# Modulation as columns, later modulation loads first, every second low part's sum on GpSimd: the start of a retention / attention / expert layer

## Chip, cores and metric

One core of one Trainium2 chip. The metric is the device time of one execution in microseconds; for the kernel before the change the median of three runs is given. TensorE is the matrix engine, VectorE, ScalarE and GpSimd (POOL in the profile) are the others, and SyncE (SP) issues most of the loads.

## What is computed

One layer over 512 latent tokens and 256 context tokens of width 1024: adaptive norm, one projection into retention and differential attention, gated merge, then a top-4-of-32 mixture of experts. The change touches only its first lines:

```python
mod_l = (jax.nn.silu(c) @ w_mod + b_mod)[:, None, :]        # c: (1, 1024), w_mod: (1024, 6144)
mod_c = (jax.nn.silu(c_ctx) @ w_mod + b_mod)[None, None, :]
sh_a, sc_a, g_a, sh_f, sc_f, g_f = jnp.split(mod_l, 6, axis=-1)
csh_a, csc_a, ... = jnp.split(mod_c, 6, axis=-1)
hl = _rmsnorm(x, norm1_g) * (1.0 + sc_a) + sh_a             # 512 rows
hc = _rmsnorm(ctx, norm1_g) * (1.0 + csc_a) + csh_a         # 256 rows
... = _project(hl, w_in); ... = _project(hc, w_in)          # everything else hangs on these
```

## The kernel before, in words

All values are float32. Large products are made from split operands: ScalarE rounds a tile to a high part (`whi` of weights, `hhi` of activations), VectorE subtracts it from the tile to get the low part (`wlo`, `hlo`), and TensorE adds high by high, high by low and low by high. `hhi` and `hlo` hold the normed, modulated activations, transposed: eight chunks k of 128 channels, 768 token columns each.

The engines run their own programs, which are written out by hand and tied by semaphores. There is no planner: the order in each engine's program is the order of the work. The start-up goes like this.

- **SyncE** loads the conditioning vectors and the identity, then four pieces of `w_mod` (`load_mod`, L563; a piece is 512 rows by 512 columns, 1 MB; two pieces make 512 columns of shift or scale), then six tiles of x and the context (`load_x`, L568). Then come the first query weights (`load_qk(0, 0)`, issued at L550), pieces 4 to 7 (each waits until the product four earlier has freed its buffer), the first key weights, and a piece for the later modulation vectors (L580).
- **TensorE** (`mod_product`, through the helper `mm` at L2089) makes each piece's product with the two conditioning columns `ct` as the stationary operand and 512 columns of `w_mod` moving: four matmuls into a 2x512 row pair, in full float32, so that the trace shows two records for each. After products 0 to 3 it transposes four tiles of x (`turn_x_tile`, L2193: eight 128x128 transposes a tile). Then it turns the first half of the modulation (`turn_mod`, L2201: eight transposes of 2x128), makes product 4, transposes the last two tiles, makes products 5 to 7, and turns the second half. After that it starts the first query projection (`head_qk(0, 0)`). This asks for the first low weights (`lo_made`) and, chunk by chunk, for `h_lo`: six matmuls a chunk.
- **VectorE** scales the tiles of x (`x_norm`, L1372), adds the bias to the product rows (`mod_row`, L1368) and copies the turned columns into `mcols` (`mod_columns`, L1419 and L1420). For each chunk k it makes scale times x plus shift in full precision (L1431, two instructions: 512 latent and 256 context columns) and subtracts the high part (L1435). Between the two halves of four chunks it makes the low part of the first weights (`lo`, L1345).
- **ScalarE** makes the sums of squares (L939), copies the transposed x out (L945), makes `hhi` (L965, L967) and the high weights (L929).
- **GpSimd** loads the bias and the norm's weights at the start, makes the reciprocal roots (L772, L774), then issues the loads of constants (`more_inputs`, L752 to L761: 0.9 MB and many small ones), and clears an accumulator once all eight `h_lo` are made (L783).

Products alternate between the first four channel chunks (products 0 to 3) and the last four (4 to 7); each half needs a shift pair and a scale pair.

Of the kernel before, what the change touches and what calls it, by code (L numbers as in the profile page):

```python
# [27 lines left out]
ALU = mybir.AluOpType  # L28
# [3 lines left out]
P = 128  # L32
D = 1024
KC = D // P
L = 512
# [202 lines left out]
def build(nc, a, scratch):  # L238
    mod_d, h2_d, list_d, acc_d, accr_d = scratch
    ctx = ExitStack()  # L240
    with ctx:
# [57 lines left out]
        mod_turned = sem("mod_turned")  # L299
# [17 lines left out]
        mod_rows = sem("mod_rows")  # L317
# [219 lines left out]
        def _(sp):  # L537
# [54 lines left out]
            load_qk(0, 0)  # L592
            for j in range(MOD_SLOTS, MOD_N):
                load_mod(j)
            load_qk(0, 1)
# [136 lines left out]
        def _(pool):  # L732
# [44 lines left out]
            for k in range(3):  # L777
                pool.wait_ge(x_sq, 2 * k + 2)
                rstd(ss[:, 2 * k:2 * k + 2], 2, D, st, out=rs[:, 2 * k:2 * k + 2], m0=2 * k).then_inc(x_rstd, 1)
            more_inputs()  # L780
            pool.wait_ge(mod_vec, 2)
# [554 lines left out]
        def _(dve):  # L1336
# [26 lines left out]
            bm = F(A_BMOD, MOD_A, COL)  # L1363

            def mod_row(n):
                c = MOD_COLS[n]
                dve.wait_ge(mod_used, 2 * n + 2)
                V.tensor_tensor(bm[0:2, c, :], ps[0:2, c, :], bm[0:2, c, :], ALU.add).then_inc(mod_rows, 1)  # L1368

# [45 lines left out]
            def mod_columns(n):  # L1415
                ks = slice(KH * n, KH * n + KH)
                dve.wait_ge(mod_turned, n + 1)
                turned = ps[:, 3 * n, 0:4 * KH].rearrange("p (s k a) -> p s a k", s=2, a=2)
                V.tensor_copy(mcols[:, 0:4:2, ks], turned[:, 0])  # L1419
                V.scalar_tensor_tensor(out=mcols[:, 1:4:2, ks], in0=turned[:, 1], scalar=1.0,  # L1420
                                       in1=mcols[:, 4, ks].unsqueeze(1).broadcast_to((P, 2, KH)),
                                       op0=ALU.add, op1=ALU.mult).then_inc(mod_vec, 1)
# [3 lines left out]
            def h_low(k):  # L1426
                xt = F(A_XT, KC, T)[:, k, :]
                if k >= 2:
                    dve.wait_ge(h_lo, k - 1)
                for s, (n0, n1) in enumerate(((0, L), (L, T))):  # L1430
                    st.did(V.tensor_scalar(tm[:, k % 2, n0:n1], xt[:, n0:n1],  # L1431
                                           mcols[:, 2 * s + 1, k:k + 1], mcols[:, 2 * s, k:k + 1], ALU.mult, ALU.add))
                dve.wait_ge(h_hi, k + 1)
                st.wait()
                V.tensor_tensor(hlo[:, k, :], tm[:, k % 2, :], hhi[:, k, :].bitcast(F32), ALU.subtract).then_inc(h_lo, 1)  # L1435
# [4 lines left out]
            mod_row(0)  # L1440
            mod_row(1)
            x_norm(4)
            x_norm(5)
            for half_k in range(2):
                if half_k:
                    mod_row(2)
                    mod_row(3)
# [639 lines left out]
        def _(pe):  # L2087
# [91 lines left out]
            def mod_product(j):  # L2179
                pe.wait_ge(e_loaded[j % MOD_SLOTS], 16 * (j // MOD_SLOTS + 1))  # L2180
                for kq in range(KH):
                    kk = KH * (j % 2) + kq
                    last = mm(ps[0:2, MOD_COLS[j // 2], :], ct[:, :, kk], mod_slot[j % MOD_SLOTS][:, kq, :], kk == 0, kk == KC - 1)
# [13 lines left out]
            def turn_mod(n):  # L2197
                pe.wait_ge(mod_rows, 2 * n + 2)
                for m in range(2 * KH):
                    col = (MOD_COLS[2 * n + m // KH] * KH + m % KH) * P  # L2200
                    last = pe.transpose(ps[:, 3 * n, 2 * m:2 * m + 2], F(A_BMOD, 2 * D)[0:2, col:col + P],  # L2201
                                        ident[0:2, 0:2])
                last.then_inc(mod_turned, 1)

# [4 lines left out]
            turn_mod(0)  # L2209
# [5 lines left out]
            turn_mod(1)  # L2215
# [582 lines left out]
```

## Time and profile before

| | |
|---|---|
| median of 3 runs | 2324.55 us (2322.3 to 2326.19) |
| the profiled execution | 2324.45 us |
| its span, first to last instruction | 2322.7 us |
| busy: TensorE, its weight loads | 98%, 78% |
| busy: VectorE, ScalarE, GpSimd | 73%, 53%, 16% |
| mean granted TensorE clock | 0.992 of full speed |

The span is what the profile covers; the profiled execution took 1.75 us more around it. Busy times are shares of the span. PE is TensorE's matmuls and PEld its weight loads, which overlap them. The chain of waits is followed back from the last instruction, at each step to what released it. A timeline row gives start, duration, engine, line, operation, tiles written and read, partitions by elements, and a count; where a row merges several records, the duration reaches to the end of the last one. The ends of matmuls are modelled, so starts are the better measure.

### The profile page before, as it was taken

How to read it: one execution, taken by the hardware profiler on the slowest of the kernel's cores; microseconds unless marked ns; L12 is line 12 of the kernel's file. 1: busy time of each engine (PE TensorE's matmuls, PEld its weight loads, DVE VectorE, ACT ScalarE, POOL GpSimd, SP SyncE). 2: the span in 40 equal slices, each digit the busy share in tenths (PEclk: the TensorE clock that was granted, in tenths of full speed). 3: DMA queues.
4: the chain of work that ended last, by engine and by line, in shares of the span. 5: the costliest groups of instructions: out<-in, count | busy, mean ns of one | idle time of the engine just before them, and what ended most of it. 6: DMA issues, size and time to landing. Idle time of an engine off the chain costs nothing.

```text
span 2322.7 us, 29938 instructions
## 1 busy us (share of the span) xinstructions
PE 2275.3 (98%) x10487; PEld 1802.7 (78%) x10487; DVE 1697.1 (73%) x1544; ACT 1222.1 (53%) x1136; POOL 377.7 (16%) x327
## 2 busy tenths in 40 slices
PE   7999999999999999999799999999999999999997
PEld 3858778686887787788678888888888888888886
DVE  4535344353636766856799999999999999999996
ACT  4212222121233723732577777777777777777774
POOL 2000000000203023000621212212211122121112
PEclk9999999999999999999799999999999999999999
DMA  8322313132231021054699999999999999999995
GB/s 294 118 91 91 127 37 128 54 123 77 73 111 52 1 91 55 1 168 161 238 378 385 370 370 379 368 375 373 374 364 371 363 370 378 367 373 376 369 372 180
DMA packets 135509, 542.89 MB, mean 234 GB/s; under 512 B 16131, under 2 KB 24467, under 8 KB 101390
## 3 DMA queue, kind: packets, MB, share of 16 engines
q1 hardware_dynamic: 123192, 516.30, 58.8%
q0 software_dynamic: 11952, 21.44, 3.8%
q10 hardware_dynamic: 296, 4.21, 0.5%
q8 instruction: 45, 0.74, 0.1%
q14 instruction: 24, 0.20, 0.0%
HBM read 533.79 MB, written 26.38 MB: 241 GB/s over the span
## 4 chain that ended last, share of the span: by engine, by line
PE 95%; DVE 1%; DMA 1%; ACT 1%; issue 0%; ACTq 0%; POOLq 0%; SPq 0%; DVEq 0%
PE ps L2089 91%; PE ps L2605 1%; PE ps L2616 1%; DMA raw<-in_w_mod 1%; PE ps L2407 1%; PE ps L2349 0%; DVE nmx L1696 0%; PE ps L2295 0%; DMA raw<-in_exp_w 0%; DMA ar<-h_d,ar 0%; ACT ar L1111 0%; PE ps L2425 0%; DVE hlo L1435 0%; PE ps L2504 0%; DVE ar L1431 0%
## 5 line engine op out<-in xcount | busy, mean ns | idle before, releaser
L2089 PE MATMUL ps<-whi,yhi 128*128 128x512 f32 x1072 | 348.5, 395 | 5.6 <-DVE yhi L2000 5.6
L2089 PE MATMUL ps<-hhi,yhi 128*128 128x512 f32 x1072 | 342.6, 389 | 0.0
L1913 DVE TENSOR_TENSOR hlo<-raw,hhi 128x2048 fp32r<-128x2048 f32 x132 | 302.4, 2292 | 48.5 <-ACT hhi L1231 48.5
L1231 ACT ACTIVATE whi<-raw 128x2048 fp32r<-128x2048 f32 x132 | 253.3, 1920 | 97.2 <-PE ps L2089 97.0
L1913 DVE TENSOR_TENSOR wlo<-raw,whi 128x2048 fp32r<-128x2048 f32 x132 | 298.8, 2284 | 4.9 <-ACT whi L1231 3.5
L1231 ACT ACTIVATE hhi<-raw 128x2048 fp32r<-128x2048 f32 x132 | 253.1, 1917 | 86.1 <-PE ps L2089 75.0
L1345 DVE TENSOR_TENSOR wlo<-raw,whi 128x2048 fp32r<-128x2048 f32 x56 | 128.2, 2289 | 219.3 <-ACT whi L929 219.3
L2089 PEld LDWEIGHTS ps<-whi,yhi 128*128 128x128 f32 x1072 | 202.6, 189 | 59.7 <-issue 12.1
L2089 PE MATMUL ps<-ar 128*128 128x128 f32 (+4 forms) x1014 | 237.5, 429 | 6.1 <-ACT ar L1145 1.4
L2089 PE MATMUL ps<-whi,hhi 128*128 128x512 f32 x592 | 233.7, 395 | 0.0
L2089 PEld LDWEIGHTS ps<-hhi,yhi 128*128 128x128 f32 x1072 | 201.2, 188 | 41.8
L2089 PE MATMUL ps<-whi,hlo 128*128 128x512 f32 x592 | 230.8, 390 | 0.0
L2089 PE MATMUL ps<-wlo,hhi 128*128 128x512 f32 x592 | 230.5, 389 | 0.0
L2089 PEld LDWEIGHTS ps<-ar 128*128 128x128 f32 (+1 forms) x1014 | 145.8, 192 | 92.5 <-issue 70.9
L929 ACT ACTIVATE whi<-raw 128x2048 fp32r<-128x2048 f32 x56 | 107.2, 1915 | 209.5 <-PE ps L2089 208.9
L2089 PE MATMUL ps<-wlo,yhi 128*128 128x512 f32 x544 | 213.1, 392 | 0.0
L2089 PE MATMUL ps<-hlo,yhi 128*128 128x512 f32 x544 | 211.7, 389 | 0.0
L2089 PE MATMUL ps<-whi,ylo 128*128 128x512 f32 x544 | 177.3, 395 | 1.9 <-DVE ylo L2019 1.9
L2089 PE MATMUL ps<-hhi,ylo 128*128 128x512 f32 x544 | 174.9, 390 | 0.6 <-DVE hlo L1913 0.5
L875 POOL DMA_INDIRECT out_x<-ar,cur x32 | 92.7, 2896 | 501.4 <-DVE ar L2029 468.8
L1913 DVE TENSOR_TENSOR wlo<-ar,whi 128x2048 fp32r<-128x2048 f32 x66 | 151.2, 2292 | 27.2 <-ACT whi L1231 27.1
L1231 ACT ACTIVATE whi<-ar 128x2048 fp32r<-128x2048 f32 x66 | 126.8, 1921 | 55.0 <-PE ps L2089 53.4
(293 smaller groups left out, 3962.8 us busy)
## 6 DMA issues: line engine op xcount, KB each, us to landing
raw<-in_exp_w SPq DMA_DIRECT2D x264, 1024.0 KB, 7.8
ar<-in_exp_w SPq DMA_DIRECT2D x132, 1024.0 KB, 7.7
raw<-in_w_in SPq DMA_DIRECT2D x44, 1024.0 KB, 5.0
raw<-in_w_mod SPq DMA_DIRECT2D x22, 1024.0 KB, 6.4
raw<-in_w_br_ret SPq DMA_DIRECT2D x8, 1024.0 KB, 5.1
ar<-in_x SPq DMA_DIRECT2D x8, 512.0 KB, 9.2
raw<-in_w_br_diff SPq DMA_DIRECT2D x4, 1024.0 KB, 5.2
raw<-in_w_out SPq DMA_DIRECT2D x4, 1024.0 KB, 10.2
```

Of the source, the lines that this page charges most:

```text
L875: pool.indirect_dma_start(a["out"], bass.IndirectOffsetOnAxis(ap=cur[:, 0:1], axis=0), F(A_Y, D), None, bounds_check=L - 1, oob_is_err=Fal ...
L929: act.activation(whi[:, j % NSPL, :, :], raw[:, s, :, :], ACT.Copy).then_inc(hi_made, 1)
L1231: act.activation(e_whi[j % ESPL], e_raw[s], ACT.Copy).then_inc(e_hi, 1)
L1345: V.tensor_tensor(wlo[:, j % NSPL, :, :], raw[:, s, :, :], whi[:, j % NSPL, :, :].bitcast(F32), ALU.subtract).then_inc(lo_made, 1)
L1913: V.tensor_tensor(e_wlo[j % ESPL], e_raw[s], e_whi[j % ESPL].bitcast(F32), ALU.subtract).then_inc(e_lo, 1)
L2089: return pe.matmul(out, lhsT, rhs, start=start, stop=stop, skip_group_check=skip)
L2407: last = pe.transpose(psf[:, TURN0 + m * P:TURN0 + (m + 1) * P], F(A_PROB, 2, 2, T)[:, u % 2, 0, m * P:(m + 1) * P], ident)
L2605: last = pe.transpose(ps[:, q, c * P:(c + 1) * P], F(A_XG, D)[:, k * P:(k + 1) * P], ident)
L2616: last = pe.transpose(ps[:, act_bank(i, hf), c * P:(c + 1) * P], F(A_AC, 2, COL)[:, hf, c * P:(c + 1) * P], ident)
```

## The change

It does three things.

1. The modulation is made as columns. In `mod_product` a 128x128 block of `w_mod` is now the stationary operand and the two columns of `ct` move: 16 matmuls a piece, into two columns each of PSUM bank 0 or 3. In odd products four more matmuls add the bias: a 2x128 piece of it is stationary and a 2x2 identity moves. The row sums on VectorE (`mod_row`) and the transposes of the rows (`turn_mod`) are gone, and `mod_columns` waits for the products themselves.
2. SyncE issues pieces 4 to 7 ahead of the first query weights.
3. GpSimd makes scale times x plus shift for chunks 1, 3, 5 and 7 (`h_parts`), into the same buffer as before. VectorE waits for it there and only subtracts. GpSimd issues the loads of constants between its two pairs of chunks, where before it issued them right after the reciprocal roots.

```diff
@@ sync @@
-            load_qk(0, 0)
             for j in range(MOD_SLOTS, MOD_N):
                 load_mod(j)
+            load_qk(0, 0)
             load_qk(0, 1)
             load_piece(0, 0)
@@ gpsimd @@
+            pool.wait_ge(x_kept, 2 * TT)
+
+            def h_parts(half_k):
+                pool.wait_ge(mod_vec, half_k + 1)
+                for k in (KH * half_k + 1, KH * half_k + 3):
+                    if k > 1:
+                        pool.wait_ge(h_lo, k - 1)
+                    hold()
+                    for s, (n0, n1) in enumerate(((0, L), (L, T))):
+                        pool.tensor_scalar(F(A_X, 2, T)[:, 1, n0:n1], F(A_XT, KC, T)[:, k, n0:n1],
+                                           mcols[:, 2 * s + 1, k:k + 1], mcols[:, 2 * s, k:k + 1],
+                                           ALU.mult, ALU.add).then_inc(h_part, 1)
+
+            h_parts(0)
             more_inputs()
+            h_parts(1)
@@ vector @@
-            def mod_row(n):
-                c = MOD_COLS[n]
-                dve.wait_ge(mod_used, 2 * n + 2)
-                V.tensor_tensor(bm[0:2, c, :], ps[0:2, c, :], bm[0:2, c, :], ALU.add).then_inc(mod_rows, 1)
 ...
-                dve.wait_ge(mod_turned, n + 1)
+                dve.wait_ge(mod_used, (n + 1) * MOD_N // 2)
 ...
-                for s, (n0, n1) in enumerate(((0, L), (L, T))):
-                    st.did(V.tensor_scalar(tm[:, k % 2, n0:n1], xt[:, n0:n1],
-                                           mcols[:, 2 * s + 1, k:k + 1], mcols[:, 2 * s, k:k + 1], ALU.mult, ALU.add))
+                if k % 2:
+                    dve.wait_ge(h_part, k + 1)
+                else:
+                    for s, (n0, n1) in enumerate(((0, L), (L, T))):
+                        st.did(V.tensor_scalar(tm[:, 0, n0:n1], xt[:, n0:n1],
+                                               mcols[:, 2 * s + 1, k:k + 1], mcols[:, 2 * s, k:k + 1], ALU.mult, ALU.add))
 ...
-            mod_row(0)
-            mod_row(1)
             x_norm(4)
             x_norm(5)
             for half_k in range(2):
-                if half_k:
-                    mod_row(2)
-                    mod_row(3)
                 mod_columns(half_k)
@@ tensor @@
             def mod_product(j):
                 pe.wait_ge(e_loaded[j % MOD_SLOTS], 16 * (j // MOD_SLOTS + 1))
+                n, part = divmod(j // 2, 2)
+                cols = [slice(2 * (KH * part + m), 2 * (KH * part + m) + 2) for m in range(KH)]
+                if j % 2:
+                    pe.wait_ge(s_norm, 16 * 2)
+                    for m in range(KH):
+                        c0 = (MOD_COLS[j // 2] * KH + m) * P
+                        mm(ps[:, 3 * n, cols[m]], F(A_BMOD, 2 * D)[0:2, c0:c0 + P], ident[0:2, 0:2], False, False, True)
                 for kq in range(KH):
                     kk = KH * (j % 2) + kq
-                    last = mm(ps[0:2, MOD_COLS[j // 2], :], ct[:, :, kk], mod_slot[j % MOD_SLOTS][:, kq, :], kk == 0, kk == KC - 1)
+                    for m in range(KH):
+                        last = mm(ps[:, 3 * n, cols[m]], mod_slot[j % MOD_SLOTS][:, kq, m * P:(m + 1) * P], ct[:, :, kk],
+                                  j % 4 == 0 and kq == 0 and m == 0, j % 4 == 3 and kq == KH - 1 and m == KH - 1, True)
                 last.then_inc(mod_used, 1)
 ...
-            def turn_mod(n):
-                pe.wait_ge(mod_rows, 2 * n + 2)
-                for m in range(2 * KH):
-                    col = (MOD_COLS[2 * n + m // KH] * KH + m % KH) * P
-                    last = pe.transpose(ps[:, 3 * n, 2 * m:2 * m + 2], F(A_BMOD, 2 * D)[0:2, col:col + P],
-                                        ident[0:2, 0:2])
-                last.then_inc(mod_turned, 1)
-
             for j in range(4):
                 mod_product(j)
             for t in range(4):
                 turn_x_tile(t)
-            turn_mod(0)
             mod_product(4)
             turn_x_tile(4)
             turn_x_tile(5)
             for j in range(5, MOD_N):
                 mod_product(j)
-            turn_mod(1)
```

## Rows read from the trace of the kernel before

**Rows 1.** The page: span, busy time, and the chain's shares by engine.

```profile
span 2322.7 us, 29938 instructions
PE 2275.3 (98%) x10487; PEld 1802.7 (78%) x10487; DVE 1697.1 (73%) x1544; ACT 1222.1 (53%) x1136; POOL 377.7 (16%) x327
...
PE 95%; DVE 1%; DMA 1%; ACT 1%; issue 0%; ACTq 0%; POOLq 0%; SPq 0%; DVEq 0%
```

**Rows 2.** The chain of waits in order of time: start, us, what.

```profile
14.78 16.83 DMA raw<-in_w_mod
...
46.15 2.28 DVE wlo L1345
48.44 1.20 DVE ar L1368 x2
...
49.68 0.65 PE ps L2201 x8
50.34 127.76 PE ps L2089 x508
```

**Rows 3.** Timeline of the weight loads, 0 to 76 us.

```profile
11.30 0.13 PEld L2089 LDWEIGHTS ps<-raw,ct 128*2 128x2 f32 x1 [0.73 <-issue]
12.15 0.13 PEld L2089 LDWEIGHTS ps<-raw,ct 128*2 128x2 f32 x1 [0.73 <-issue]
...
13.30 0.09 PEld L2089 LDWEIGHTS ps<-raw,ct 128*2 128x2 f32 x1 [0.34 <-issue]
13.73 0.09 PEld L2089 LDWEIGHTS ps<-raw,ct 128*2 128x2 f32 x1 [0.34 <-issue]
...
25.16 1.73 PEld L2193 LDWEIGHTS ps<-cst,ar 128*128 128x128 f32 x16 [1.05 <-DVE ar L1372]
...
49.68 0.57 PEld L2201 LDWEIGHTS ps<-cst,ar 2*128 2x128 f32 x8 [2.69 <-DVE ar L1368]
```

**Rows 4.** Stretches: us, busy (records) of PE, PEld, DVE, ACT, POOL; clock; DMA; GB/s.

```profile
26.40:29.80 3.40, 2.53 (x22) 2.08 (x21) 2.60 (x4) 3.40 (x8) 0.46 (x1) 1.00 1.07 371
...
46.80:50.30 3.50, 1.74 (x12) 0.69 (x10) 2.83 (x3) 0.00 (x0) 0.00 (x0) 0.99 0.32 69
50.30:53.70 3.40, 3.40 (x9) 2.75 (x9) 2.82 (x7) 3.06 (x5) 0.00 (x0) 0.50 1.00 392
...
1111.70:1115.10 3.40, 2.66 (x22) 2.27 (x20) 3.25 (x8) 1.32 (x3) 0.00 (x0) 1.00 0.13 38
1115.20:1118.50 3.30, 2.72 (x12) 2.63 (x12) 2.28 (x8) 0.21 (x1) 2.78 (x4) 0.50 0.14 50
```

**Rows 5.** Timeline of TensorE's matmuls, 0 to 76 us.

```profile
9.64 11.97 PE L2089 MATMUL ps<-raw,ct 128*2 128x512 f32 x24 [5.88 <-DMA raw<-in_w_mod]
21.45 3.60 PE L2089 MATMUL ps<-ar,ct 128*2 128x512 f32 x8
...
44.33 3.60 PE L2089 MATMUL ps<-ar,ct 128*2 128x512 f32 x8 [0.22 <-DMA ar<-in_w_mod]
```

**Rows 6.** Timeline of TensorE's matmuls, 1080.5 to 1084 us.

```profile
1081.35 1.87 PE L2089 MATMUL ps<-ar,mcols 128*128 128x32 f32 x16
1083.05 1.07 PE L2504 MATMUL ps<-cst,ar 128*128 128x128 f32 x8
```

**Rows 7.** Timeline of the weight loads, 1115.3 to 1131 us.

```profile
1115.46 2.63 PEld L2089 LDWEIGHTS ps<-ar 128*128 128x128 f32 x12 [1.25 <-ACT ar L1220]
...
1128.89 1.56 PEld L2605 LDWEIGHTS ps<-cst,ar 128*128 128x128 f32 x8 [0.26 <-issue]
```

**Rows 8.** Timeline of TensorE's matmuls, 1106 to 1150 us.

```profile
1111.61 0.39 PE L2089 MATMUL ps<-hhi,hlo 128*128 128x512 f32 x1
1111.84 1.64 PE L2089 MATMUL ps<-ar 128*128 128x4 f32 x14
```

**Rows 9.** Groups of instructions by line, shapes kept apart.

```profile
L797 POOL TENSOR_TENSOR ar<-ar 128x512 f32<-128x512 f32 x20 | 24.0, 1202 | 98.5 <-ACT ar L1012 98.5
...
L1435 DVE TENSOR_TENSOR hlo<-ar,hhi 128x768 fp32r<-128x768 f32 x8 | 7.7, 959 | 1.9 <-ACT hhi L967 0.8 <-DVE ar L1431 0.5
```

More of the change, by code:

```diff
@@ L298, in build @@
         mod_stored = sem("mod_stored")
-        mod_turned = sem("mod_turned")
+        h_part = sem("h_part")
         s_init = sem("s_init")
@@ L316, in build @@
         c_made = sem("c_made")
-        mod_rows = sem("mod_rows")
         x_sq = sem("x_sq")
@@ L1361, in _ @@
             V.tensor_scalar(ct[:, :, :], ct[:, :, :], 0.5, None, ALU.mult).then_inc(c_made, 1)
-            bm = F(A_BMOD, MOD_A, COL)
-            def mod_row(n):
-                c = MOD_COLS[n]
-                dve.wait_ge(mod_used, 2 * n + 2)
-                V.tensor_tensor(bm[0:2, c, :], ps[0:2, c, :], bm[0:2, c, :], ALU.add).then_inc(mod_rows, 1)
             def x_norm(t):
```

## The prediction

> **What bounds the kernel now.** I read the page first: TensorE is busy 98% of the span and is 95% of the chain of waits [rows 1]. A change pays, or costs, by what it does to TensorE's line. Then I followed the chain in order of time: from 50.34 us TensorE's own products carry it without a break [rows 2]. Before that lies the start-up, the only part that the change touches. Its pieces: the fifth modulation weight lands at 31.61 (14.78 + 16.83), the split of the first query weights holds VectorE until 48.43, two row sums take it to 49.64, eight small transposes to 50.33, and the projections begin [rows 2]. So the question is when TensorE can begin the first projection. Call this T: now 50.3 us. What stands behind T is dependent work and moves with it one for one.
>
> Two more readings. First, a product of the old form is eight records, 3.4 us from start to start; its weights are two columns and its 512 moving columns set the time. The loads of its weights are 0.85 us apart before 12.2 us and 0.43 us apart from 13.3 us [rows 3]: the granted clock is recorded as full there, but the spacing says 1.2 GHz first, then 2.4 GHz. The clock is also at 0.50 for 3.4 us after T [rows 4]. Second, the timeline of TensorE: products 0 to 3 run from 9.6 to 25.05, product 7 starts at 44.33 as its weights land [rows 5].
>
> **The new product, step by step.** Now the 128x128 block of modulation weights is loaded as stationary operand and only two columns move. One 1 MB piece takes 16 such matmuls, 32 records. The nearest rows: 16 records with 128x128 weights and 32 moving columns take 1.70 us from their start to the next group's (1081.35 to 1083.05), 0.106 us each at 2.4 GHz [rows 6]. At 1.2 GHz, 12 such weight loads take 2.63 us, 0.219 each [rows 7]; I take twice 0.106, 0.213. So a product costs 32 x 0.106 = **3.4 us at 2.4 GHz**, what it costs now, but 32 x 0.213 = **6.8 us at 1.2 GHz**. Everything hangs on the clock.
>
> **Which clock.** The windows [rows 4] say what TensorE did before it fell. From 26.4 to 29.8 it was busy 2.53 of 3.40 us, with 128-column transposes, weight loads 2.08 us: clock 1.00, kept. From 1111.7 to 1115.1 it was busy 2.66 us, weight loads 2.27 us, a little more of both; but almost all of it moved 4 columns a record, the last 512-column record having started at 1111.61 [rows 8]. There the clock fell, and the next stretch runs at 0.50. That stretch is busy 2.72 of 3.30 us with 32-column records and the clock does not rise [rows 4]. Before T the same: 1.74 us busy, of it the last of a product and eight two-column transposes, and it fell. [...] The new products move two columns a record, from a start at 1.2 GHz. I take them to run at 1.2 GHz unless transposes of x have just raised the clock.
>
> The Trainium skill (TensorE: Matmul & The Clock Gate, section LDWEIGHTS) gives a weight load as columns divided by 1.2 GHz, with no word of the gate: an estimate of 107 ns at either level, with which a product would cost 3.4 us throughout and nothing be lost. The trace agrees at the high level (0.106) and differs at the low one (0.219), and the measurement decides.
>
> **Bias.** Each odd product gets four matmuls with 2x128 weights, eight records. Bounds: the two-row transposes, 0.57/8 = 0.071 at 2.4 GHz [rows 3], and the full load's 0.106. Doubled at 1.2 GHz: 0.14 to 0.213, 1.1 to 1.7 us a group. The load has the same 128 columns and is a plain matmul's, so 0.213: 1.7 us (0.85 at 2.4 GHz).
>
> **T by this path.** Products 0 to 3: 9.6 + 4 x 6.8 + 2 x 1.7 = 40.2 (25.05 before). Then 32 transposes of x. Loads of transposes take 0.195 each at 1.2 GHz [rows 7] and 0.108 (16 in 1.73) at 2.4 [rows 3]. Unbroken, full-width work raised the clock after some 3.4 us behind T; I allow 5 us at the low level, 24 transposes, and 8 more at the high one, 0.9: 46.1. Product 4 still rides on that: 3.4, to 49.5. Sixteen transposes, between 1.7 and 3.4: 2.6, to 52.1. Product 5 with bias between 5.7 (clock falling inside it) and 8.5: 7.1, to 59.2. Product 6: 6.8, to 66.0. Product 7 with bias 8.5: **T = 74.5**. That is 24.2 us later than 50.3. Bounds: the clock rising early and falling late in this stretch, T = 71; all of it at 1.2 GHz, 9.6 + 8 x 6.8 + 4 x 1.7 + 48 x 0.213 = 81.
>
> **What the change saves.** Four row sums and both turns of the modulation leave the path: 1.20 and 0.65 us of the chain before T [rows 2]. They are replaced by nothing behind product 7, as the projection waits only for its weights' split and the first columns; this gain is already in T, since I rebuilt it. **Loads moved ahead:** pieces 4 to 7 lose 1 MB in front of them. At the 371 GB/s of [rows 4] that is 2.8 us earlier at 31.6 and 44.3. It is worth nothing on the new path, because TensorE reaches piece 4 at 46 and piece 7 at 66, and each issue waits for a product four earlier. The query weights land later than before, but are split long before T. If products were fast this cover is gone and the rival below counts it. GpSimd's queue: the constants' loads are issued behind the first two GpSimd sums. These wait for the last transposes (52.1) and for VectorE's second low part, so the loads go out near 58 us. VectorE asks for them behind its last low part, near T + 8 = 82, and 24 us cover loads of under 1 MB. They also leave the window of the modulation loads, worth nothing for the same reason. **GpSimd's sums:** its nearest row is a two-input 128x512 product, 1.20 us [rows 9]; 768 columns cost 1.8 by that rate, and no less than VectorE's subtraction of the same width, 0.96 [rows 9]. The chain for the last chunk is T + 0.35 + 2 x (1.8 + 0.96) = T + 5.9. TensorE wants it after 42 matmuls at 0.25 (127.76 us for 508 [rows 2]): T + 10.5. Hidden; it would show above 4.1 us a pair. VectorE is freed of 0.9 us a chunk, worth nothing there. The 3.4 us at half clock behind T stay, their length uncertain by 1 us of cost either way.
>
> Sum: 24.2 on the profiled execution's 2324.45 = 2348.65; the median, 2324.55, is 0.1 above. **I forecast 2349**, its own range 2345 to 2353.
>
> **Rivals.**
> *All at 1.2 GHz.* Transposes do not raise the clock from the low level. For it: eight of them, 1.56 us, left it at half clock near 1129 [rows 7]; against: they kept it at 26.4 to 29.8. T = 81, time 2355. The Trainium skill (TensorE: Matmul & The Clock Gate, Part 4) says that transposes do not count as busy; the trace disagrees as to keeping the clock, and shows nothing long enough as to raising it. Chance 0.12.
> *The clock holds once raised.* Back-to-back small matmuls hold what transposes gained: product 4 to 49.5, 1.7, 4.25, 3.4, 4.25 to T = 63.1, time 2337. Against it speaks the fall at 1115.1. Chance 0.10.
> *Not slower: unbroken small matmuls count as busy.* The rows in which the clock fell had gaps of a quarter; the new stream has none. The place is the first 4 us of product 0; if the clock rises there, products cost 3.4. Products 0 to 3 end at 26.8, transposes 31.7, product 4 35.1, transposes 37.1, then 4.25, 3.4 and 4.25: T = 49.0, all weights landed thanks to the moved load, and the split of the query weights ends about 47. Gain 1.3, and 1.7 more if no half-clock stretch follows T: 2321.5 to 2323. The point from which it decides: a loss begins once more than about 1.5 us of products runs at the low level. Chance 0.18.
>
> **How the numbers follow.** Forecast 0.56, the other three 0.12, 0.10, 0.18, unnamed 0.04. About 0.2% (4.65 us) is what a measurement of this kernel can tell. Only the forecast and the first two rivals pass it, slower 0.79. The last rival lies within it: same 0.19. Even T = 48 with no slow stretch gives 2320.4, so faster 0.02. Leaving out the last rival and the unnamed, the range runs from the held clock, 2335, to all low, 2357.
>
> **What would show it.** In the new profile: granted clock 0.50 in most of 10 to 75 us, weight loads of w_mod 0.21 us apart, product 4's start near 46, the first projection matmul near 74, VectorE and GpSimd idle before it. A clock of 1.00 with loads 0.106 apart in product 1 makes me wrong by 26 us; GpSimd pairs above 4.1 us, or a wait of the projection on the low parts, would make the smaller steps wrong.

## The result and the profile after

The kernel after the change takes 2355.77 us (median of four runs, 2348.55 to 2357.33) against 2323.82 us before (four runs, 2322.3 to 2326.19): ratio 1.0131, 95% interval 1.0119 to 1.0143. It is **slower by 1.3%**; forecast were 2349 us and a range of 2335 to 2357. The profiled execution of after took 2356.62 us, 32.2 more than that of before.

The page of after, its span, its busy times, and the chain's shares by engine:

```profile
span 2354.8 us, 30361 instructions
PE 2310.3 (98%) x10695; PEld 1862.1 (79%) x10695; DVE 1692.3 (72%) x1532; ACT 1222.4 (52%) x1136; POOL 379.6 (16%) x335
...
PE 97%; DVE 1%; issue 1%; ACT 0%; DMA 0%; POOLq 0%; DVEq 0%; SPq 0%; POOL 0%; ACTq 0%
```

Against [rows 1] TensorE is busy 35.0 us more, for 208 more records, and holds 97% of the chain instead of 95%. VectorE lost 4.8 us of work and nothing came of it. So the time went where it was looked for, onto TensorE's line. Its timeline from the start to T, the first matmul of the first query projection:

```profile
9.71 6.96 PE L2094 MATMUL ps<-ct,raw 128*128 128x2 f32 x32 [5.92 <-DMA raw<-in_w_mod]
16.60 1.87 PE L2094 MATMUL ps<-cst,ar 2*128 2x2 f32 x8
18.39 13.81 PE L2094 MATMUL ps<-ct,raw 128*128 128x2 f32 x64
32.14 1.87 PE L2094 MATMUL ps<-cst,ar 2*128 2x2 f32 x8
33.93 6.99 PE L2094 MATMUL ps<-ct,ar 128*128 128x2 f32 x32
40.78 6.18 PE L2207 MATMUL ps<-cst,ar 128*128 128x128 f32 x32
46.80 4.53 PE L2094 MATMUL ps<-ct,raw 128*128 128x2 f32 x32
51.19 3.65 PE L2207 MATMUL ps<-cst,ar 128*128 128x128 f32 x16
54.77 1.86 PE L2094 MATMUL ps<-cst,ar 2*128 2x2 f32 x8
56.56 13.81 PE L2094 MATMUL ps<-ct,raw 128*128 128x2 f32 x64
70.31 1.86 PE L2094 MATMUL ps<-cst,ar 2*128 2x2 f32 x8
72.11 6.99 PE L2094 MATMUL ps<-ct,ar 128*128 128x2 f32 x32
78.95 0.77 PE L2094 MATMUL ps<-hhi,whi 128*128 128x512 f32 x1
```

TensorE waits for nothing after 9.71 us: no line but the first has an idle time. Two products (64 records) take 13.75 us from start to start, 6.87 each, where the old product took 3.4; [rows 5] are the same stretch before. The four groups of eight with 2x2 are the bias, 1.79 each. T is 78.95 us instead of 50.34 (50.27 as the timeline of before has it), **28.6 us later**. The weight loads show the level of the clock (start, us):

```profile
9.68 6.90 PEld L2094 LDWEIGHTS ps<-ct,raw 128*128 128x128 f32 x32 [6.00 <-issue]
```

32 loads in 6.90 us are 0.216 us apart, the spacing of [rows 7] (0.219), which is 1.2 GHz, not that of [rows 6] (0.106). The stretches around the fast piece and around T (us, busy and records of PE, PEld, DVE, ACT, POOL; granted clock; DMA; GB/s):

```profile
45.00:50.00 5.00, 5.00 (x41) 5.00 (x39) 1.56 (x4) 3.36 (x7) 0.89 (x2) 0.93 0.70 234
50.00:55.00 5.00, 5.00 (x24) 4.67 (x24) 0.00 (x0) 1.92 (x4) 0.00 (x0) 0.50 0.49 163
70.00:75.00 5.00, 5.00 (x24) 4.97 (x24) 0.00 (x0) 0.00 (x0) 0.00 (x0) 0.50 0.00 0
...
80.00:85.00 5.00, 5.00 (x16) 3.95 (x15) 4.00 (x6) 5.00 (x9) 3.75 (x4) 0.66 0.93 322
```

Read the row of 70 to 75: TensorE is busy every moment, its weight loads 4.97 of 5 us, and the clock is at 0.50. Nothing else in the core works there, no transfer either. Only from about 46 to 49.3 us, behind 24 transposes or so, does this start-up see 2.4 GHz.

**Behind T.** The offset between the two kernels is 28.6 us at T, 29.1 at the end of the first chain of products (207.24 against 178.10), because the stretch at half clock behind T is 4.5 us long instead of 3.4, and 29.4 at the last transposes of the experts' end. The last 2.8 us come at one gap near the end. The first matmul behind it, in after and then in before (timeline of TensorE; the idle time stands in brackets):

```profile
2330.80 0.79 PE L2094 MATMUL ps<-whi,ylo 128*128 128x512 f32 x1 [3.38 <-issue]
```

```profile
2299.95 0.49 PE L2089 MATMUL ps<-whi,ylo 128*128 128x512 f32 x1 [1.90 <-DVE ylo L2019]
```

VectorE makes the awaited operand in 1.28 us in both, from 2298.44 to 2299.72 before and from 2327.81 to 2329.09 after. TensorE goes on 0.23 us later before and 1.71 us later after, and then at half clock:

```profile
2328.00:2330.00 2.00, 0.00 (x0) 0.00 (x0) 1.09 (x2) 2.00 (x3) 1.20 (x1) 0.85 0.00 0
2330.00:2332.00 2.00, 1.20 (x3) 1.02 (x4) 1.93 (x1) 1.70 (x1) 0.38 (x1) 0.50 0.39 41
```

Before, the same gap passed at a clock of 1.00. At the first matmul behind the gap after is 1.5 us further behind than in front of it, and at the end of the span 2.8. But the longer gap is not a price by itself. From where TensorE stops (2298.05 us before, 2327.42 in after) to the end of the span it is 24.6 us before and 27.4 in after. Three of the runs below have the long gap too (3.28, 3.04 and 2.84 us), but the clock at 1.00 in it and behind it, and there the same stretch takes 24.8, 24.6 and 24.6 us. Before, TensorE has to wait again a little later:

```profile
2305.25 0.50 PE L2089 MATMUL ps<-hhi,ylo 128*128 128x512 f32 x1 [0.54 <-DVE hlo L1913]
```

Behind a long gap this wait is gone, since VectorE made `hlo` meanwhile. So a late start costs 0.2 us at most where the clock holds, and the 2.8 us are the half clock: it lasts until about 2336.2, and 5.4 us of TensorE's work at 0.50 lose 2.7. The sum over the two profiles is 28.6 + 0.5 + 0.3 + 2.8 = 32.2 us. What makes the gap longer is the subject of the last three experiments.

### The profile page after: what moved, and what is told of

Its sections match the earlier page's. It is cut to its first block, busy times and chain, and to the rows that moved or that the text cites. A ratio compares the mean times of both kernels' runs of the same rounds, so it can differ in the third digit from the quotient of the medians.

```text
span 2354.8 us, 30361 instructions
## 1 busy us (share of the span) xinstructions
PE 2310.3 (98%) x10695; PEld 1862.1 (79%) x10695; DVE 1692.3 (72%) x1532; ACT 1222.4 (52%) x1136; POOL 379.6 (16%) x335
## 4 chain that ended last, share of the span: by engine, by line
PE 97%; DVE 1%; issue 1%; ACT 0%; DMA 0%; POOLq 0%; DVEq 0%; SPq 0%; POOL 0%; ACTq 0%
PE ps L2094 92%; PE ps L2609 1%; PE ps L2620 1%; PE ps L2411 1%; PE ps L2207 0%; PE ps L2353 0%; DMA raw<-in_w_mod 0%; DVE nmx L1701 0%; PE ps L2299 0%; ACT ar L1125 0%; DVE wlo L1918 0%; PE ps L2429 0%; PE ps L2508 0%; DVE yhi L2005 0%; DVE ar L1714 0%
```

## The experiments

### The change taken apart: column products alone, the rest alone

The first run (its edit is against after) has only the new products: the first query weights are loaded ahead of the later modulation weights as before, VectorE forms all sums, GpSimd issues the constants' loads as before.

```
-            for j in range(MOD_SLOTS, MOD_N):
-                load_mod(j)
             load_qk(0, 0)
+            for j in range(MOD_SLOTS, MOD_N):
+                load_mod(j)
...
-            h_parts(0)
             more_inputs()
-            h_parts(1)
...
-                if k % 2:
-                    dve.wait_ge(h_part, k + 1)
-                else:
-                    for s, (n0, n1) in enumerate(((0, L), (L, T))):
+                for s, (n0, n1) in enumerate(((0, L), (L, T))):
```

> The column products alone: the load order and VectorE's sums are those of the kernel before. Clock theory (the products run at 1.2 GHz and TensorE's line is the whole loss): first projection matmul at 79 us as in the changed kernel, time within 2 us of its 2356. Rival (the moved loads and GpSimd's sums carry part of the loss, for example the 3 us behind T): 3 us or more faster than 2356, with the first projection matmul before 77 us.

Measured: 2351.37 us (2351.16 to 2356.89, four runs), ratio 1.0119 [1.0104, 1.0135]. The profiled execution, 2356.89 us, has T at 79.06:

```profile
79.06 0.77 PE L2076 MATMUL ps<-hhi,whi 128*128 128x512 f32 x1
```

Its timeline up to T stays within 0.3 us of that of after. The expected T (79) came, the expected time (within 2 us of 2356) did not: the median is 4.4 us under that of after, while the two profiled executions differ by 0.3. The intervals of the two ratios overlap, and both kernels have runs near 2350 and near 2357, so four runs of each can't tell whether the two smaller steps cost anything. The products carry the loss: all of it by the profiles, 27 us by the medians.

The second run is the complement, on the kernel before: the loads moved and GpSimd's sums, the row products kept. The third leaves the loads where they were too, so that only GpSimd's sums and, behind them, the later issue of the constants are new.

```
-            load_qk(0, 0)
             for j in range(MOD_SLOTS, MOD_N):
                 load_mod(j)
+            load_qk(0, 0)
...
+            h_parts(0)
             more_inputs()
+            h_parts(1)
```

> The moved loads and GpSimd's sums alone, with the old row products. Clock theory: product 4 starts up to 2.8 us earlier (31.65 before), the granted clock is 1.00 from product 1 on, first projection matmul between 47 and 50 us, time 2320 to 2324. Rival (GpSimd's sums or the later constants' loads hold the first chunks): first projection matmul after 51 us and a time above 2325.

> GpSimd's sums and the later constants' loads alone, old products, old load order. Theory (what the row-product kernel with both gained, 1.8 us, comes from earlier modulation weights): at most 1.5 us of it here, because only the small constants' transfers leave the window; product 7 starts between 43.7 and 44.3, time 2322.4 to 2324.2. Rival (GpSimd's sums are the gain): 2322.4 or less.

Measured: 2322.37 us (2320.86 to 2323.84, eleven runs), ratio 0.9992 [0.9983, 1.0001], with the loads moved; 2321.87 us (2321.21 to 2323.45, eleven runs), ratio 0.9991 [0.9982, 1.0], without. The end of the start-up in the third run, and the stretch behind T:

```profile
48.76 0.65 PE L2220 MATMUL ps<-cst,ar 2*128 2x2 f32 x8 [1.14 <-DVE ar L1384]
49.34 0.51 PE L2108 MATMUL ps<-hhi,whi 128*128 128x512 f32 x1
```

```profile
49.30:52.70 3.40, 3.40 (x17) 2.77 (x17) 2.12 (x5) 2.98 (x5) 3.36 (x7) 1.00 1.10 258
```

VectorE, freed of two sums, reaches the row sums earlier: TensorE's wait before the last turn is 1.14 us instead of 1.8 and T is 49.34, 1.0 us earlier than before. Where [rows 4] had half clock behind T, the clock is 1.00. With the loads moved T is 49.03 (2320.6 us of span against 2320.0): the move adds nothing that can be measured. For the second run T and the time are what the clock theory expected. For the third run the theory (earlier weights are the gain) expected 2322.4 us or more and missed; its rival, that GpSimd's sums are the gain, held. At most these two parts give back 0.1%, about the edge of what the measurement tells from nothing. In after they can't give even that, since T there does not wait for VectorE.

### Is it the clock? Wide work mixed into the products

A product costs 6.87 us either because TensorE runs at 1.2 GHz, or because such a matmul costs 0.21 us a record here whatever the clock. The first try was to keep the clock up: one matmul of 512 moving bf16 columns and two stationary ones ahead of each modulation matmul, 128 in all, into a bank that is not yet used.

```
+                        mm(ps[0:2, 1, :].rearrange("p (a n) -> p a n", a=2), ident.bitcast(BF16)[:, 0:2],
+                           ident.bitcast(BF16).unsqueeze(1).broadcast_to((P, 2, 2 * P)), True, True)
                         last = mm(ps[:, 3 * n, cols[m]], mod_slot[j % MOD_SLOTS][:, kq, m * P:(m + 1) * P], ct[:, :, kk],
```

> The changed kernel with work added: ahead of each of the 128 modulation matmuls TensorE makes a bf16 matmul with 512 moving columns (the identity, into a spare bank; its result is read by nobody). Clock theory: the clock is 1.00 from about 13 us on, weight loads of w_mod 0.11 to 0.2 us apart, first projection matmul between 50 and 63 us, time 2326 to 2338, so 18 us or more faster than the changed kernel although it does more. Rival (the records cost 0.215 us for another reason than the clock, for example the strided columns or the many short accumulations): nothing becomes faster, 128 x 0.21 us are added, first projection matmul at or after 79 us, time 2356 to 2383.

Measured: 2428.38 us (2425.2 to 2432.71), ratio 1.0453 [1.0437, 1.0469]. **A miss of both expectations**: the wide work did not raise the clock, and the run is 45 us above the rival's upper bound.

```profile
10.49 0.59 PE L2094 MATMUL ps<-cst 128*2 128x512 bf16 x1
11.01 0.59 PE L2094 MATMUL ps<-ct,raw 128*128 128x2 f32 x2
```

```profile
130.00:140.00 10.00, 10.00 (x33) 6.37 (x34) 0.00 (x0) 0.00 (x0) 0.00 (x0) 0.50 0.00 0
```

Filler and pair take 0.517 us each, the clock stays at 0.50 in products 0 to 3, and a product grows from 6.87 to 16.5 us. Only behind the 32 transposes of x is the clock at 1.00, and there, from 84.8 to 89.7 us, in product 4, filler and pair take 0.31 us each:

```profile
85.46 0.38 PE L2094 MATMUL ps<-cst 128*2 128x512 bf16 x1
85.77 0.38 PE L2094 MATMUL ps<-ct,raw 128*128 128x2 f32 x2
```

So the pair's time goes with the clock here too, but mixed with the filler's. As a test of the bare products' price it was not clean. So the next run raised the clock first, and left the products alone: 13 of the same wide matmuls before product 0, in the time in which TensorE waits for the first weights anyway.

```
+            for _ in range(13):
+                mm(ps[0:2, 1, :].rearrange("p (a n) -> p a n", a=2), ident.bitcast(BF16)[:, 0:2],
+                   ident.bitcast(BF16).unsqueeze(1).broadcast_to((P, 2, 2 * P)), True, True)
             pe.wait_ge(c_made, 3)
```

> The changed kernel with 13 bf16 matmuls of 512 moving columns ahead of product 0, while TensorE waits for the first weights (3.8 to 9.7 us). Clock theory (wide unbroken work raises the clock, the column products lose it): product 0 begins at 2.4 GHz, its weight loads 0.107 us apart for 2 to 4 us, then 0.215 again; first projection matmul 1.5 to 4 us earlier than 78.95, the rest as it was. Rival (the small matmuls cost 0.215 whatever the clock): product 0 takes 6.9 us, nothing changes.

Measured: 2353.9 us (2351.12 to 2354.24, four runs), ratio 1.0125 [1.0109, 1.014]; profiled 2353.66 against after's 2356.62.

```profile
3.83 5.51 PE L2094 MATMUL ps<-cst 128*2 128x512 bf16 x13
9.27 4.14 PE L2094 MATMUL ps<-ct,raw 128*128 128x2 f32 x32
13.34 1.86 PE L2094 MATMUL ps<-cst,ar 2*128 2x2 f32 x8
```

```profile
9.70:12.00 2.30, 2.30 (x23) 2.30 (x22) 1.92 (x12) 0.00 (x0) 0.00 (x0) 1.00 1.02 332
12.00:14.00 2.00, 2.00 (x12) 1.98 (x13) 1.69 (x12) 0.00 (x0) 0.00 (x0) 0.61 1.04 385
14.00:16.00 2.00, 2.00 (x10) 1.98 (x11) 0.49 (x6) 0.00 (x0) 0.00 (x0) 0.50 1.05 389
```

This is the cleanest reading of the study. The same 32 records take 4.07 us here (9.27 to 13.34) and 6.89 in after (9.71 to 16.60). While the clock is 1.00, 23 of them pass in 2.3 us; when it falls, near 12.4 us, with TensorE busy without a gap, ten take 2.0. T comes at 75.71, 3.2 us earlier (0.4 of it because product 0 begins earlier), and the profiled time is 3.0 less. The cost of the products is the clock's, and in this run the unbroken products lose the clock that they are given.

The last of this kind joins both: the 13 ahead, and a wide matmul ahead of each narrow pair.

```
+            for _ in range(13):
+                mm(ps[0:2, 1, :].rearrange("p (a n) -> p a n", a=2), ident.bitcast(BF16)[:, 0:2],
+                   ident.bitcast(BF16).unsqueeze(1).broadcast_to((P, 2, 2 * P)), True, True)
...
+                        mm(ps[0:2, 1, :].rearrange("p (a n) -> p a n", a=2), ident.bitcast(BF16)[:, 0:2],
+                           ident.bitcast(BF16).unsqueeze(1).broadcast_to((P, 2, 2 * P)), True, True)
                         last = mm(ps[:, 3 * n, cols[m]], mod_slot[j % MOD_SLOTS][:, kq, m * P:(m + 1) * P], ct[:, :, kk],
```

> The kernel with a 512-column filler ahead of every modulation matmul (2428 us, clock never raised), with the same 13 wide matmuls ahead of product 0. Theory that such a mix can hold a raised clock but not raise it: every product at 2.4 GHz, one filler and its pair 0.52 us where it was 1.03, first projection matmul near 85 us, time 2355 to 2365, some 65 us faster for 13 more matmuls. Rival (the mix loses the clock as the column products do): 2 to 5 us faster than 2428.

Measured: 2426.04 us (2425.27 to 2429.24), ratio 1.0441 [1.0425, 1.0457].

```profile
12.40 0.38 PE L2094 MATMUL ps<-ct,raw 128*128 128x2 f32 x2
12.71 0.52 PE L2094 MATMUL ps<-cst 128*2 128x512 bf16 x1
13.16 0.59 PE L2094 MATMUL ps<-ct,raw 128*128 128x2 f32 x2
```

Starts are 0.31 us apart up to 12.71 and 0.52 behind it: the mixture loses the clock within 0.5 us of the moment at which the bare products did. The rival's 2 to 5 us under 2428 came. Behind the transposes the mixture ran 4.9 us at 1.00 before the fall, the bare product 4 of after 2.5. Wide matmuls in equal number with narrow ones neither raise nor hold the clock here, and each costs as much as the pair that it was to help.

### How much of it is the bias?

This kernel leaves the bias `b_mod` out of shift and scale.

```
-                if j % 2:
-                    pe.wait_ge(s_norm, 16 * 2)
-                    for m in range(KH):
-                        c0 = (MOD_COLS[j // 2] * KH + m) * P
-                        mm(ps[:, 3 * n, cols[m]], F(A_BMOD, 2 * D)[0:2, c0:c0 + P], ident[0:2, 0:2], False, False, True)
```

> The changed kernel without the sixteen bias matmuls; it leaves the bias b_mod out of shift and scale. Clock theory: 4 x 1.79 us less at the low clock, first projection matmul near 72 us, time 2349. Rival (the bias matmuls lie beside other work): no change, 2356.

Measured: 2339.64 us (2339.43 to 2347.3, four runs), ratio 1.008 [1.0065, 1.0095]: 16.1 us under after's median, where 7.2 were expected. T is 65.85.

```profile
43.13 3.63 PE L2094 MATMUL ps<-ct,raw 128*128 128x2 f32 x32
46.63 1.94 PE L2202 MATMUL ps<-cst,ar 128*128 128x128 f32 x16
48.41 10.76 PE L2094 MATMUL ps<-ct,raw 128*128 128x2 f32 x64
59.02 6.96 PE L2094 MATMUL ps<-ct,ar 128*128 128x2 f32 x32
```

```profile
43.10:46.60 3.50, 3.50 (x34) 3.50 (x33) 1.56 (x4) 1.98 (x5) 0.88 (x2) 1.00 0.61 193
...
59.00:65.80 6.80, 6.80 (x33) 6.80 (x34) 0.00 (x0) 0.00 (x0) 3.93 (x8) 0.50 0.40 82
```

The four groups are worth 7.2 us, 4 x 1.79. The expectation (T near 72, time 2349) had only these. The rest of the 13.1 us of T is the clock: product 4 passes wholly at 1.00 (3.50 us against 4.39), the 16 transposes take 1.78 instead of 3.58, and products 5 and 6 take 10.61 instead of 13.75; product 0 begins 0.5 later. Of the profiled times' 17.1 us (2356.62 against 2339.54), 2.8 are the gap near the end, which is 1.90 us here as before, with full clock in it and behind it, and about 0.9 a half-clock stretch behind T of 2.8 us instead of 4.5; 0.3 are not placed. So the moments at which the clock rises and falls, which no line of the code sets, are worth some 6 us of T on one path. The two rows of one product, 3.50 us at 1.00 and 6.8 at 0.50, are also the direct measure of the forecast's 3.4 and 6.8.

### Keeping the row products: can the rest be made to pay?

Since row products cost no clock, the last try kept them and went after what stands before T: GpSimd's sums, ScalarE's and VectorE's split of the first query weights moved ahead of the last copies of x and the low parts, and the second turn of the modulation behind the first chunk of the projection, so that TensorE need not stand still for the row sums. The main edit:

```
-            turn_mod(1)
+            pe.wait_ge(mod_rows, 3)
...
+                    if h == 0 and s == 0 and kk == 0:
+                        turn_mod(1)
```

> Old row products and old load order, GpSimd's sums and later constants kept; the split of the first query weights moves into the pause of ScalarE and VectorE before the last tiles of x, and the second turn of the modulation behind the first chunk of the query projection. Theory (TensorE's line up to product 7 is the bound): first projection matmul between 47 and 48.5 us at 1.00, time 2319.5 to 2322. Rival (VectorE's chain of the second half is too late: a wait of the projection on a low part takes back what the start gains): TensorE idle inside the first query projection, time 2322 to 2325.

Measured: 2321.96 us (2321.45 to 2323.66, eleven runs), ratio 0.9992 [0.9983, 1.0001].

```profile
47.91 0.50 PE L2111 MATMUL ps<-hhi,whi 128*128 128x512 f32 x1
...
49.49 0.65 PE L2223 MATMUL ps<-cst,ar 2*128 2x2 f32 x8
...
61.17 0.50 PE L2111 MATMUL ps<-hhi,whi 128*128 128x512 f32 x1 [0.91 <-DVE wlo L1364]
```

T is 47.91, 2.4 us earlier than before, at full clock. Of this the turn takes back 0.6 inside the projection, and TensorE then waits 0.91 us for the low part of the next weights, which VectorE makes behind its last low part. The start went forward, VectorE's chain did not: T and the time are what the theory expected, and the wait that its rival expected is there too. The three versions with row products stand at 0.9991 to 0.9992 of before: one result three times, at the edge of what can be told from no change. None is a version to put in the kernel's place on this evidence, though none is slower.

### The gap near the end: TensorE's code

In after, TensorE goes on 1.5 us later than its operand allows. In the transfers of that stretch there is one packet only between 2328.1 and 2330.5 us, and it is code (queue and kind: packets, MB, share of 16 engines; stretch 2330.1 to 2330.5):

```profile
q8 instruction: 1, 0.02, 16.8%
```

TensorE goes on at 2330.80. With column products alone, in the run with the 13 ahead and in both with mixed wide matmuls, the gap is 3.24, 2.99, 3.04 and 2.84 us, and such a packet starts 0.3 to 0.5 us before its end each time.

By itself this tells little, since in the kernel before, with its gap of 1.90 us, one starts 0.5 us before the end too (at 2299.48). What differs is when it comes, counted from where TensorE stops: 2.5 to 2.9 us later in all six profiles with a long gap, those of the next kernels included; 1.4 to 1.7 us later in the five with a gap of 1.90 to 2.06 us that have it inside; and 0.4 to 0.5 us earlier in the run without bias and in one below, both with 1.90. VectorE's operand is there after 1.67 us, in after as before. All thirteen gap lengths fit with TensorE going on when it has both, the operand and, 0.3 to 0.5 us behind the start of its packet, the code.

That the queue is TensorE's is shown by its count of packets on the page of the profile: 45 before, 46 in the two runs below in which nothing but TensorE's program grew. In the mixed runs the gap is long though the clock stays at 1.00, so the falling clock does not make the gap. In the program the gap's end is the first work behind the loop over the experts and the blocks that are skipped when no more work is left, so jumps stand just ahead of it.

Three kernels test the other cause, where in its program TensorE stands: tiny bf16 matmuls, two stationary and two moving columns, ahead of product 0, in the idle time before the first weights.

```
+            for _ in range(48):
+                mm(ps[0:2, 1, 0:2], ident.bitcast(BF16)[:, 0:2], ident.bitcast(BF16)[:, 0:2], True, True)
             pe.wait_ge(c_made, 3)
```

The first has these 48 in after, the second 80 in the kernel before, the third 48 in the kernel before.

> The kernel after with 48 tiny matmuls (two stationary and two moving bf16 columns) ahead of product 0, where TensorE waits for the first weights anyway; they add 96 TensorE instructions and nothing to the path. In question is the gap near the end: 3.38 us in after against 1.90 before, and half clock behind it, 2.8 us together. Theory, TensorE's code: a packet of the instruction queue lands 0.4 to 0.6 us before TensorE goes on in every long gap (after, column products alone, both runs with wide matmuls and the burst), but 2.5 us before it in the run without bias, whose gap was short. Against the kernel before, after has 208 more TensorE records, each with a weight load, so 416 instructions; the run without bias 352. In steps of 256 these are 160 and 96, the kernel before 0. With 96 more, after stands at 512, the place of the kernel before: gap 1.90, clock 1.00 behind it, 2.8 us less, near 2353. Rival, the start-up: the gap is longer because the clock or the timing of the start-up differs; nothing changes: gap 3.0 to 3.4, 2356.

> The kernel before with 80 of the same tiny matmuls ahead of product 0: 160 more TensorE instructions, the place of after in steps of 256. T stays at 50.3 (range 49.3 to 50.5) since they end before the first weights are there. Code theory: the gap near the end grows from 1.90 to about 3.4 us, and the clock falls in it or not: 1.5 to 2.8 us slower than before, 2325.5 to 2327. Rival: gap 1.90, the time of before within 1 us.

> The control to the other: the kernel before with 48 tiny matmuls, 96 instructions, the place of the run without bias. Both theories: gap 1.90 us, the time of before within 1 us; a longer gap here would say that the tiny matmuls as such disturb the end, or that the count of instructions does not set it.

Measured: after with 48, 2351.64 us (2348.88 to 2354.22, four runs), ratio 1.0119 [1.0102, 1.0136]; before with 80, 2327.02 us (2325.46 to 2329.73, ten runs), ratio **1.0016 [1.0007, 1.0026]**; before with 48, 2323.42 us (2321.41 to 2325.73, ten runs), ratio 0.9999 [0.9989, 1.0008]. The first matmul behind the gap, in this order:

```profile
2327.11 0.49 PE L2094 MATMUL ps<-whi,ylo 128*128 128x512 f32 x1 [2.06 <-DVE ylo L2024]
```

```profile
2302.17 0.49 PE L2089 MATMUL ps<-whi,ylo 128*128 128x512 f32 x1 [3.28 <-issue]
```

```profile
2296.92 0.49 PE L2089 MATMUL ps<-whi,ylo 128*128 128x512 f32 x1 [1.90 <-DVE ylo L2019]
```

Adding instructions to after shortens the gap, adding 160 to before makes it as long as after's, adding 96 leaves it. The tiny matmuls take 1.34 us (48) and 2.14 us (80), well inside the idle time. So where its code lies sets how long TensorE's gap is, with nothing of the change in the kernel.

What it costs is less than the medians suggest. In after with 48 the stretch from where TensorE stops to the end is 24.6 us, 2.8 less than in after. The profiled executions differ by 5.2 us, because T is 76.89 as well, 2.1 earlier, behind a clock that rose earlier; the expectation did not have this. In before with 80 the clock stayed at 1.00 in the gap and behind it, and the stretch takes 24.8 us, 0.2 more than before. The median is 3.6 us over its control's, and the profiled executions (2325.46 and 2321.41, each the fastest of its ten) are 4.1 apart; but of these 3.9 are there before TensorE reaches the gap (2298.89 against 2295.02). T is 51.20 us, outside the expected 49.3 to 50.5, against 50.08 in the control, and a stretch at half clock follows it that the control lacks. Why is open. So late code is shown to lengthen the gap, and not to make the kernel before slower. The Trainium skill (Runtime: NRT & Kernel Launch, Instruction fetch mechanics) says that code comes in 16 KiB blocks of 256 instructions, and that a taken branch whose target is outside the loaded pages waits for a fetch; the packet's 0.02 MB agrees with it, and so do the counts of TensorE's matmul and load records that were added to those of before. Less whole steps of 256, they are 0 or 96 in the seven profiles with 1.90 to 2.06 us and 160 or 186 in the six with 2.84 to 3.38. Which jump it is was not tried.

## Why the prediction was right

The outcome (slower, by the products at half clock, hidden by nothing) and its mechanism hold; the sum was 7 us short of the median. The measured time lies outside the forecast's own 2345 to 2353 and inside the whole range of 2335 to 2357, whose upper part was there for the rival with everything at 1.2 GHz: that it holds the number is partly luck. Step by step:

- **"I take them to run at 1.2 GHz unless transposes of x have just raised the clock."** Held, in both halves. In the run with the wide matmuls ahead the clock falls near 12.4 us behind narrow products without a gap, so the gaps in the rows of before were not needed for a fall. The rows bear less than the prediction read into them: of the 22 records from 1111.7 to 1115.1 us, 14 move 4 columns, but two move 32 and four are 128-column transposes, with idle time behind them; at T the clock fell with 1.76 us of idle time in the stretch. They did not separate narrow work from idle time; the run did. The rival "unbroken small matmuls count as busy" (2321.5 to 2323) fell with it.
- **The price of a product**, 6.8 and 3.4 us: measured 6.87, and 3.50 in the run without bias. 0.1 short on each slow product.
- **The bias**, 1.7 a group: 1.79. The upper of the two bounds was the right one.
- **Products 0 to 3 end at 40.2**: 40.78.
- **Transposes to 46.1**: 46.80; 6.0 us for 32, forecast 5.9. That they raise the clock from the low level was an assumption; it held, near 46 us.
- **What then rides on the high clock is the term that was mis-sized.** Product 4 was put at 3.4 and took 4.39, the 16 transposes at 2.6 and took 3.58, product 5 with its bias at 7.1 and took 1.79 + 6.87 = 8.66. The clock fell about 2.5 us into product 4, while the forecast let it last through product 4 and into product 5. Together 3.5 of the 4.45 us by which T came late (78.95 against 74.5). The run without bias shows the longer hold that was forecast, so the size was not unreasonable, only not dependable.
- **"What stands behind T moves with it one for one"**: true to 0.8 us over 2200 us of dependent work, but for the 2.8 us of half clock that begin in the gap near the end, which no step of the prediction had. It priced the new instructions by their time and not by where they push the code behind them; that this made the gap longer is shown, that the longer gap made the clock fall is not (it fell in three of six such profiles). Terms of T 4.4, behind T 0.8 and tail 2.8 make the 8.0 us between the forecast for the profiled execution (2348.65) and its time (2356.62).
- **All at 1.2 GHz, 2355 us**: nearer in number, wrong in mechanism. It would have needed 6.8 us for the 32 transposes and half clock at 45 to 50 us, where 6.0 us and 0.93 are read. The Trainium skill (TensorE: Matmul & The Clock Gate, Part 4) says that the full clock does not engage for transposes, which do not count as busy in the same way; here the clock rose near 46 us behind 5 us of nothing but transposes, and the measurement decides.
- **The clock holds once raised, 2337 us**: wrong, it fell in product 4.
- **Moved loads, worth nothing**: shown twice. In after no product waits for its weights, and in the row versions the move changes nothing measurable.
- **GpSimd's sums hidden**: the last low part's row stands below. A pair takes 2.28 to 2.53 us where 1.8 was taken (0.96 to 1.8 were the bounds): over the upper bound, under the 4.1 at which it would show.

```profile
79.62 2.45 POOL L788 TENSOR_SCALAR ar<-ar,mcols 128x512 f32<-128x512 f32 x2 [10.57 <-DVE mcols L1427]
```

```profile
85.70 0.96 DVE L1445 TENSOR_TENSOR hlo<-ar,hhi 128x768 fp32r<-128x768 f32 x1 [0.52 <-POOL ar L788]
```

The last low part ends at 86.66, T + 7.7, where T + 5.9 was forecast and T + 10.5 the deadline; TensorE, itself at half clock up to 83.4 us, does not wait. VectorE's own subtraction takes 1.18 instead of 0.96 us in places. The constants' loads go out at 61.67, forecast 58, and nothing waits for them.

## What to carry to other kernels

Swapping operands so that wide weights are loaded and a few columns move can cost the same at full clock and yet double in time, where the clock is at its lower level behind the new form (3.5 us a product at 1.00, 6.87 at 0.50): price each form at both levels, and look in the trace for a stretch in which narrow matmuls alone ran. When the start-up's clock is unsettled, give the forecast a range of several microseconds for it. Every edit also moves the code behind it: a gap that changes far downstream, behind a loop, may be code that arrives late, and a few idle instructions put in or taken out tell. Then compare the stretch from the gap to the end, not the gap: here 1.4 us more of gap cost 0.2 at full clock. What relieves an engine that nobody waits for (VectorE here) is worth nothing.

## What was not expected of the hardware

- TensorE's code can come late: the same gap lasts 1.90 to 2.06 us or 2.84 to 3.38 us, by the number of instructions ahead of it (three kernels made to show it). Up to the end of the span this costs 0.2 us at most while the clock holds. With the long gap the clock fell inside it in three of six profiles (after, column products alone, 13 wide ahead), and the stretch to the end is 2.6 to 2.8 us longer. With the short one it fell behind the gap in two of seven (sums on GpSimd with the loads moved, and with the split moved), and the stretch is 0.4 us longer.
- Alternating matmuls of 512 bf16 columns with pairs of records of two fp32 columns cost 0.517 us each at half clock and 0.31 at full, and did not keep TensorE at full speed though it was busy throughout.
- 48 tiny bf16 matmuls take 1.34 us, 0.028 us each, and do not move the clock: product 0 behind them takes 6.9 us.
- In after the recorded clock is 1.00 from the start to 49 us, while the weight loads stand 0.216 us apart up to 40 us: ahead of its first change the record says nothing, and the spacing of the loads has to be read instead.
